# The feed-forward of an encoder layer in two stages, its inner activations passing through DRAM

## The reference

```python
x = x + gate1 * mix
h2 = rmsnorm(x, g_ffn) * (1 + scale2) + shift2
ff = (jax.nn.silu(h2 @ w_gate) * (h2 @ w_up)) @ w_down      # D_FF = 2816 = 22 tiles of 128
return x + gate2 * ff
```

## Time and profile before

| | |
|---|---|
| time, three runs | 1761.38, 1762.17 (median), 1762.43 us |
| the profiled execution | 1760.1 us, its span from first to last instruction 1758.3 us |
| mean granted TensorE clock | 0.999 of full speed |
| TensorE busy | 1718.3 us (98% of the span) |
| VectorE, ScalarE, GpSimd busy | 803.3, 440.5, 528.6 us |
| DRAM read, written | 98.51, 9.45 MB |

### The profile page before, as it was taken

How to read it: one execution, slowest core, us unless ns; L and a number is a source line. 1 busy time by engine, 2 the same in 40 slices (tenths; PEclk the granted TensorE clock), 3 DMA queues, 4 the chain that set the end, 5 groups by cost and what they waited for, 6 DMA issues and landing times.

```text
span 1758.3 us, 21827 instructions
## 1 busy us (share of the span) xinstructions
PE 1718.3 (98%) x8293; PEld 1370.7 (78%) x8293; DVE 803.3 (46%) x1235; ACT 440.5 (25%) x830; POOL 528.6 (30%) x431
## 2 busy tenths in 40 slices
PE   5999999999999999999999999999999999999998
PEld 1668888766768887888888888888888888888887
DVE  3705885078775364252515243242615243342525
ACT  4412332288761144101010111101010211111010
POOL 1301220188546553050504022040505031140505
PEclk9999999999999999999999999999999999999999
DMA  9751013154113101101100101110110101011013
GB/s 380 265 205 36 24 34 69 42 113 79 49 65 127 37 1 60 37 24 37 36 26 21 48 24 36 36 36 24 36 36 12 48 24 40 32 36 35 24 36 143
DMA packets 99311, 108.69 MB, mean 62 GB/s; under 512 B 19655, under 2 KB 82337, under 8 KB 95929
## 3 DMA queue, kind: packets, MB, share of 16 engines
q1 hardware_dynamic: 97401, 104.82, 19.0%
q10 hardware_dynamic: 1728, 3.15, 0.5%
q0 software_dynamic: 128, 0.02, 0.0%
HBM read 98.51 MB, written 9.45 MB: 61 GB/s over the span
## 4 chain that ended last, share of the span: by engine, by line
PE 78%; issue 1%; DVE 1%; ACT 0%; DMA 0%; POOL 0%; DVEq 0%; ACTq 0%; POOLq 0%
PE banks L101 23%; PE banks L102 23%; PE banks L103 23%; PE banks L989 2%; PE banks L1019 2%; PE banks L1325 2%; PE banks L998 2%; PE banks L1006 1%; PE banks L975 1%; PE banks L1790 1%; PE banks L1308 0%; DMA wff_raw<-in_w_up 0%; DVE alt L1231 0%; PE banks L1753 0%; PE banks L1336 0%
## 5 line engine op out<-in xcount | busy, mean ns | idle before, releaser
L1744 POOL TENSOR_TENSOR x<-x,ff_scratch 128x512 f32<-128x512 f32 x198 | 263.5, 1363 | 798.4 <-DVE ff_scratch L1636 797.8
L101 PE MATMUL banks<-h_hi,wff_hi 128*128 128x512 f32 x1056 | 411.5, 390 | 0.0
L103 PE MATMUL banks<-h_hi,wff_lo 128*128 128x512 f32 x1056 | 410.8, 389 | 0.0
L102 PE MATMUL banks<-h_lo,wff_hi 128*128 128x512 f32 x1056 | 410.8, 389 | 0.0
L1511 DVE TENSOR_TENSOR wff_lo<-wff_raw,wff_hi 128x1024 fp32r<-128x1024 f32 x66 | 81.6, 1236 | 403.7 <-ACT wff_hi L1507 403.7
L103 PEld LDWEIGHTS banks<-h_hi,wff_lo 128*128 128x128 f32 x1056 | 198.2, 188 | 41.3
L101 PEld LDWEIGHTS banks<-h_hi,wff_hi 128*128 128x128 f32 x1056 | 198.2, 188 | 41.0 <-issue 0.2
L102 PEld LDWEIGHTS banks<-h_lo,wff_hi 128*128 128x128 f32 x1056 | 198.2, 188 | 40.8
L1636 DVE TENSOR_TENSOR ff_scratch<-banks,gate 128x512 f32<-128x512 f32 x264 | 177.3, 687 | 73.8 <-PE banks L103 53.2
L101 PE MATMUL banks<-wff_hi,ff_hi 128*128 128x512 f32 x528 | 205.4, 389 | 0.0
L102 PE MATMUL banks<-wff_lo,ff_hi 128*128 128x512 f32 x528 | 205.4, 389 | 0.0
(11 more groups left out here) (173 smaller groups left out, 2096.1 us busy)
## 6 DMA issues: line engine op xcount, KB each, us to landing
ada_rest<-in_w_ada SPq DMA_DIRECT2D x16, 1024.0 KB, 7.0
wff_raw<-in_w_gate SPq DMA_DIRECT2D x22, 512.0 KB, 4.9
wff_raw<-in_w_up SPq DMA_DIRECT2D x22, 512.0 KB, 3.8
wff_raw<-in_w_down SPq DMA_DIRECT2D x22, 512.0 KB, 3.2
ada<-in_w_ada SPq DMA_DIRECT2D x8, 1024.0 KB, 16.3
win_raw<-in_w_in SPq DMA_DIRECT2D x16, 512.0 KB, 4.0
x_first<-in_x_sample SPq DMA_DIRECT2D x2, 2048.0 KB, 13.5
wo_raw<-in_w_o SPq DMA_DIRECT2D x4, 1024.0 KB, 5.0
```

Of the source, the lines that this page charges most:

```text
L101: pe.matmul(out, lhs[0], rhs[0], start=start, stop=False)
L102: pe.matmul(out, lhs[0], rhs[1], start=False, stop=False)
L103: return pe.matmul(out, lhs[1], rhs[0], start=False, stop=stop)
L1744: pool.tensor_tensor(part, part, scratch[:, n % 3], ALU.add).then_inc(d_added, 1)
```

## The change

The feed-forward is cut in two stages.

**Gate and up.** 22 units, gate and up of each pair in turn (`unit`). A unit covers two inner tiles: 256 columns of `w_gate` or `w_up`, loaded as one 1 MB transfer into one raw buffer, split in halves into one `a_hi`/`a_lo` buffer. Its six tiles (`ORDER`: both inner tiles of chunk 0, then of chunk 1, then of chunk 2) take banks 0 to 5. Silu goes to six slots in SBUF, the product replaces it in its slot, and SP stores the slot, 256 KB, in the new DRAM tensor `ff_rows` (2816 x 1536).

**Down.** 33 groups: for each chunk of 512 tokens the 11 pairs in turn (`down`). A group needs two row tiles of `w_down` and the two inner tiles of that chunk from `ff_rows`: three transfers of 512 KB (`load_down`) into one of three slots, which lie where `h_hi` and `h_lo` were. `down_hi` and `down_lo` split a slot in two instructions each, of 2048 and 1024 columns. The eight outputs of a chunk (four token tiles by two halves) hold the eight banks through all 11 groups of the chunk; each is gated and added to `x1` once, after the eleventh. SP loads group g + 3 when group g was used (`slot_used`). On VectorE the split of group g + 2 stands before the gating after group g. Outputs of a chunk are stored as halves (256 KB) during the next chunk, those of the last at the end. The down stage is written out, not looped.

Around it: the first weight tile's two splits stand elsewhere among the squares (ScalarE) and after tile 46 of `gate_mix` (VectorE); the third chunk's turns stand after each of the eight steps of the unit's second tile, in banks 6 and 7; `modulate` writes into the place of `h_lo` instead of a ring of two, which takes a wait out of it; semaphores of earlier stages are used again at higher counts.

```diff
...
+    ff_rows = nc.dram_tensor("ff_rows", (D_FF, T), F32).ap()
...
+    ORDER = [(f, c) for c in range(NCH) for f in range(2)]
...
+    f2_hi, f2_lo = (at(f"f2_{n}", [128, KT, T], F32R, off) for n, off in (("hi", H_HI), ("lo", H_LO)))
+    f2_raw = at("f2_raw", [128, KT, T], F32, H_LO)
...
+    DOWN_BANK = [6, 7, 0, 1, 2, 3, 4, 5]
...
+    def slot_used(eng, g):
+        c, jj = divmod(g, PAIRS)
+        if jj == PAIRS - 1:
+            eng.wait_ge(d_summed, DB * c + DB)
+        else:
+            eng.wait_ge(f2_used, (PAIRS - 1) * c + jj + 1)
...
+        def load_w(j, kind):
+            sp.dma_start(a_raw[:], (w_gate, w_up)[kind][:, bass.ds(j * 256, 256)].rearrange("(k p) n -> p k n", p=128)
+                         ).then_inc(raw_in, 16)
+        def load_next(j, kind):
+            u = 2 * j + kind
+            sp.wait_ge(w_ready, W0 + 2 * u + 2)
+            load_w(j + kind, 1 - kind)
+        def store_ff(j, i):
+            f, c = ORDER[i]
+            sp.wait_ge(product, 6 * j + i + 1)
+            sp.dma_start(ff_rows[bass.ds((2 * j + f) * 128, 128), CH * c:CH * c + CH], act_slot(i)).then_inc(ff_stored, 16)
+        def load_down(g):
+            c, jj = divmod(g, PAIRS)
+            s = g % 3
+            cols = slice(CH * s, CH * s + CH)
+            if g < 3:
+                sp.wait_ge(summed, done(PAIRS - 1, UP, 2 * s + 1))
+            else:
+                slot_used(sp, g - 3)
+            for f in range(2):
+                row = 128 * (2 * jj + f)
+                sp.dma_start(f2_raw[:, 2 * f:2 * f + 2, cols], w_down[row:row + 128, :].rearrange("p (h n) -> p h n", h=2)
+                             ).then_inc(f2_in[s], 16)
+            if c == 0:
+                sp.wait_ge(ff_stored, 96 * jj + 96)
+            sp.dma_start(f2_raw[:, 4:6, cols], ff_rows[256 * jj:256 * jj + 256, CH * c:CH * c + CH].rearrange(
+                "(f p) t -> p f t", p=128)).then_inc(f2_in[s], 16)
...
+        load_next(PAIRS - 1, GATE)
+        last = PAIRS - 1
+        store_ff(last, 0)
+        load_down(0)
+        store_ff(last, 1)
+        load_down(1)
+        for i in range(2, 5):
+            store_ff(last, i)
+        load_down(2)
+        store_ff(last, 5)
+        for g in range(3, GROUPS):
+            load_down(g)
...
+    def split_w_hi(act, j, kind, f):
+        act.wait_ge(raw_in, 16 * (2 * j + kind) + 16)
+        act.activation(a_hi[:, :, 128 * f:128 * f + 128], a_raw[:, :, 128 * f:128 * f + 128], ACT.Copy).then_inc(w_hi_s, 1)
+    def split_w_lo(dve, j, kind, f):
+        u = 2 * j + kind
+        dve.wait_ge(w_hi_s, W0 + 2 * u + f + 1)
+        dve.tensor_tensor(a_lo[:, :, 128 * f:128 * f + 128], a_raw[:, :, 128 * f:128 * f + 128],
+                          a_hi[:, :, 128 * f:128 * f + 128].bitcast(F32), ALU.subtract).then_inc(w_ready, 1)
+    def silu(act, j, i):
+        if i == 0 and not (isinstance(j, int) and j == 0):
+            act.wait_ge(ff_stored, 96 * j)
+        act.wait_ge(summed, done(j, GATE, i))
+        src = banks[:, i]
+        act.activation(act_slot(i), src, ACT.Silu).then_inc(silu_ready, 1)
+    def down_hi(act, g):
+        s = g % 3
+        cols = slice(CH * s, CH * s + CH)
+        act.wait_ge(f2_in[s], F2_IN0[s] + 48 * (g // 3) + 48)
+        act.activation(f2_hi[:, 0:4, cols], f2_raw[:, 0:4, cols], ACT.Copy).then_inc(f2_hi_s, 1)
+        act.activation(f2_hi[:, 4:6, cols], f2_raw[:, 4:6, cols], ACT.Copy).then_inc(f2_hi_s, 1)
+    def unit_act(act, j, kind, last):
+        for i in range(NP):
+            if kind == GATE:
+                silu(act, j, i)
+            if i >= NP - 2:
+                act.wait_ge(summed, done(j, kind, i))
+                if not last:
+                    split_w_hi(act, j + kind, 1 - kind, i - NP + 2)
+                else:
+                    down_hi(act, i - NP + 2)
...
-        split_hi(act, 0, 0)
...
+        act.wait_ge(o_summed, SEQ.index((2, TT - 1)) + 1)
+        split_w_hi(act, 0, GATE, 0)
         square(8)
-        square(9)
-        square(10)
-        split_hi(act, 0, 1)
-        square(11)
+        split_w_hi(act, 0, GATE, 1)
+        for t in range(9, 12):
+            square(t)
...
+        for g in range(2, GROUPS):
+            down_hi(act, g)
...
+    def down_lo(dve, g):
+        s = g % 3
+        cols = slice(CH * s, CH * s + CH)
+        for i, part in enumerate((slice(0, 4), slice(4, 6))):
+            dve.wait_ge(f2_hi_s, 2 * g + i + 1)
+            dve.tensor_tensor(f2_lo[:, part, cols], f2_raw[:, part, cols], f2_hi[:, part, cols].bitcast(F32), ALU.subtract
+                              ).then_inc(f2_ready, 1)
+    def unit_dve(dve, j, kind, last):
+        for i in range(NP):
             if kind == UP:
+                dve.wait_ge(summed, done(j, kind, i))
+                dve.wait_ge(silu_ready, SILU0 + 6 * j + i + 1)
+                dve.tensor_tensor(act_slot(i), banks[:, i], act_slot(i), ALU.mult).then_inc(product, 1)
+            if i >= NP - 2:
                 if not last:
+                    split_w_lo(dve, j + kind, 1 - kind, i - NP + 2)
+                else:
+                    down_lo(dve, i - NP + 2)
...
+            if m == TT * OS - 2:
+                split_w_lo(dve, 0, GATE, 0)
+        split_w_lo(dve, 0, GATE, 1)
...
+        for g in range(GROUPS):
+            if g + 2 < GROUPS:
+                down_lo(dve, g + 2)
+            c, jj = divmod(g, PAIRS)
+            if jj < PAIRS - 1:
+                continue
+            dve.wait_ge(gate2_in, 16)
+            for n in range(DB):
+                m = DB * c + n
+                t, half = divmod(m, 2)
+                cols = slice(512 * half, 512 * half + 512)
+                dve.wait_ge(d_summed, m + 1)
+                if m >= 3:
+                    waits_added(dve, m - 3)
+                dve.tensor_tensor(scratch[:, m % 3], banks[:, DOWN_BANK[n]], gate2[:, REQ[c], cols], ALU.mult).then_inc(d_gated, 1)
+                if on_dve(n):
+                    dve.wait_ge(d_gated, m + 1)
+                    dve.tensor_tensor(x1_back[:, t, cols], x1_back[:, t, cols], scratch[:, m % 3], ALU.add).then_inc(d_added_dve, 1)
...
+        def unit(j, kind):
+            u = 2 * j + kind
+            first = isinstance(u, int) and u == 0
+            for i, (f, c) in enumerate(ORDER):
+                if c == 0:
+                    pe.wait_ge(w_ready, W0 + 2 * u + f + 1)
+                if first:
+                    if i < 4:
+                        pe.wait_ge(gated, TT * OS - 3 + i)
+                    else:
+                        pe.wait_ge(t_ready, TURN0 + KT * 2)
                     if f == 0:
+                        h_ready(c)
+                elif kind == GATE:
+                    pe.wait_ge(product, 6 * (j - 1) + i + 1)
+                else:
+                    pe.wait_ge(silu_ready, SILU0 + 6 * j + i + 1)
+                for k in range(KT):
+                    last = mm3(pe, banks[:, i], [part[:, k, 128 * f:128 * f + 128] for part in (a_hi, a_lo)],
+                               [part[:, k, CH * c:CH * c + CH] for part in (h_hi, h_lo)], k == 0, k == KT - 1)
+                    if k == KT - 1:
+                        last.then_inc(summed, 1)
+                    if first and i == 1:
+                        turn(2 * KT + k)
+        def down(g):
+            c, jj = divmod(g, PAIRS)
+            s = g % 3
+            cols = slice(CH * s, CH * s + CH)
+            pe.wait_ge(f2_ready, 2 * g + 2)
+            for n in range(DB):
                 t, half = divmod(n, 2)
+                bank = DOWN_BANK[n]
+                if jj == 0 and c:
+                    pe.wait_ge(d_gated, DB * (c - 1) + n + 1)
+                elif jj == 0 and n >= 2:
+                    pe.wait_ge(product, 6 * (PAIRS - 1) + n - 1)
                 for f in range(2):
+                    last = mm3(pe, banks[:, bank], [part[:, 4 + f, CH * s + 128 * t:CH * s + 128 * t + 128] for part in (f2_hi, f2_lo)],
+                               [part[:, 2 * f + half, cols] for part in (f2_hi, f2_lo)], jj == 0 and f == 0, jj == PAIRS - 1 and f == 1)
+                if jj == PAIRS - 1:
+                    last.then_inc(d_summed, 1)
+            if jj < PAIRS - 1:
+                last.then_inc(f2_used, 1)
...
+        for g in range(GROUPS):
+            down(g)
...
```

More of the change, by code:

```diff
@@ L1396, in second_half @@
[L1396 to L1399, removed]
+    o_summed, gated, x1_added = sem("o_summed"), sem("o_gated"), sem("x1_added")
+    squared, rooted, rstd, xn_dve, xn_act = kept.squared_act, kept.rooted, kept.rstd_ready, kept.x_normed, sem("xn_act")
+    turned, t_ready, hi_ready, split_even, split_odd = (
+        kept.x_turned, kept.t_ready, kept.h_hi_ready, kept.split_even, kept.split_odd)
@@ L1484, in run_sp @@
             load_o(n)
-        load(0, 0)
-        sp.wait_ge(o_summed, TT * OS)
-        load(0, 1)
-        sp.wait_ge(gated, TT * OS)
-        load(0, 2)
```

(35 more changed lines are left out.)

412 lines of the change are left out of this document (152 added, 260 removed).

## The result

The changed kernel takes **1770.24 us** (median of 7 runs, 1766.26 to 1774.64) against 1761.66 us for the kernel before beside it (7 runs, 1760.09 to 1762.43): ratio 1.0047, 95% interval 1.0034 to 1.006. It is slower by 8.6 us. The forecast was 1767.0 us in a range of 1761.5 to 1771.0. Timed again later it took 1767.61 us against 1761.77 (5 runs; 1.0034, interval 1.002 to 1.0048).

The account below looks back on a forecast made before the run. TensorE's matmul stream was taken to set the end. Terms +5.2 (stops), +0.3 (gate-up to down), -0.2 (start), -0.5 (tail) gave +4.8 on the profiled 1760.1; with the median 2.1 higher, 1767.0 us, range 1761.5 to 1771.0.

Parts of the forecast that it names:

- Matmuls: Feed-forward on TensorE: 4752 matmuls of the same shapes at the same pitch, 1077.2 us as before, cost 0.
- removed work: Gatings and residual additions fall from 264 to 24 each; no TensorE wait names them, so gain 0.
- steady groups: Down stage inside a chunk: load, split and subtractions take 12.5 us of 21.8 available, hidden, cost 0.
- The stops: After groups 10 and 21, TensorE waits 2.5 us for gating behind loads and split; 2.6 each with restart, +5.2.
- the restart: TensorE's first matmul after a stop: 0.32 us instead of 0.23 to the second, a tenth more per stop.
- The clock behind the stops: Down stage after each chunk end: no prediction step had slow matmuls there; only the restart's tenth was priced.
- From gate-up to down: Between the stages: first group's split takes 5.42 us, TensorE comes after 5.25; with a restart +0.3 us.
- The start: First feed-forward matmul through first turn: 0.4 late plus 1.4 idle less 2.0 of present waits, -0.2 us.
- The waits behind `t_second`: TensorE waits of 0.6 us at the third chunk's turns, said to go: no ring, no silu in between.
- The tail: Kernel's end: last store is 256 KB instead of 512, 2.1 against 2.6 us, so -0.5 us.
- loads land sooner: Rival at chunk ends: loads of 5.95 us, deciding below 6.4; sum +2.5, 1764.7 us, no change; chance 0.25.
- No stops: Rival at chunk ends: gating not last, or split in time; with start's waits gone -2.5, 1759.7 us; chance 0.10.

Follow-up runs that it names:

- the filled stop: Changed kernel plus twelve matmuls with a stationary tile of zeros at the first and second chunk ends; 1765.51 us against 1767.61 for the changed kernel beside it.
- the run with two landings: Changed kernel, but the split's first part waits only for the two `w_down` loads, its second for the inner tiles' load; 1762.06 us, ratio 1.0003 to before.
- the gate-first kernel: Changed kernel with VectorE gating before splitting group g + 2 at both chunk ends: 1760.20 us; with the first weight's subtraction one tile earlier too: 1759.42 us.

## Why the prediction came out as it did

The direction and the mechanism were right: two stops, after groups 10 and 21, by the order on VectorE. Its steps in turn:

- **Matmuls, removed work, steady groups**: right. The pitch is 0.2267 us as before, the changed kernel waits in no other place, and the 4752 matmuls cost the same. 407 us less work on VectorE and GpSimd bought nothing, since no wait of TensorE hung on it.
- **The stops**: forecast 2.6 each with the restart, 5.2 together; measured 2.17 + 2.81 = 4.98. The loads of 6.74 and 7.38 us bracket the 7.07 taken from the loads of `x`.
- **The clock behind the stops**: missing. The restart was priced at a tenth of a microsecond an end, from the row of a turn, behind which the clock had not fallen; it cost 1.69 and 1.49 us here, and the filled stop, together with the DMA shares of the other stretches, shows that this is the stop's doing. The Trainium skill ("TensorE: Matmul & The Clock Gate", HAM oscillation) says that TensorE's standing still makes the clock drop in a running kernel. The trace agrees in three of the four stops of the changed kernel's two profiles, though the waits in the page's example are longer than these. It should have stood among the rivals.
- **From gate-up to down**: right, forecast +0.3, measured +0.30.
- **The start**: mis-sized. Forecast -0.2, measured 0.25 + 0.11 - 1.62 = -1.26. The waits behind `t_second` went, as said. TensorE started 0.36 later instead of 0.4: the subtraction ended at 672.10, 1.1 us after the GpSimd instruction that was running (to 671.01), so VectorE was next, as forecast, and not GpSimd's addition. But the wait at the first turn came out at 0.97 us instead of the 1.4 that were put there, and other small gaps among the turns went too.
- **The tail**: right, forecast -0.5, measured -0.58.

With the forecast's own terms the sum was +4.8; corrected by +3.2 for the clock, -0.2 for the stops, -1.1 for the start and -0.1 for the tail it is the 6.6 us of the profile. Two errors of opposite sign, +3.2 and -1.1, partly cancelled; that the sum is better than its parts is luck. The median of the first seven runs is 3.2 us above the forecast, that of the second five 0.6; how much of this is the scatter of the part ahead and how much the clock behind the stops was read in two profiles only.

Of the rivals, "loads land sooner" would have needed less than 6.4 us; the rows gave 6.7 to 8.6, and the run with two landings shows what it would have brought. "No stops" is the gate-first kernel: 1.2 us faster than before by the medians (interval to no difference at all), where the rival said 2.5. In its profile the start gives 1.26 us and the tail some 0.6, with 0.30 lost from gate-up to down; that is 1.6, and no other place of its feed-forward differs from before. The gate-first kernels are the best of this study, and hold at most 0.2% over the kernel before.

## What to carry to other kernels

On an engine that works in program order, hand the next consumer its buffers first and prefetch afterwards: the same instructions in the other order at two places out of 33 were worth 8 us here. When TensorE sets the time, a stop can cost more than its length (here up to 2.7 us of slow matmuls behind it), so look at the granted clock of the stretch behind it and not only at the waits. Work taken from engines that TensorE doesn't wait for is worth nothing until a wait names it.

## What was not expected of the hardware

- After stops of 2.17, 2.52, 2.81, 4.02 and 5.46 us between dense matmuls the granted clock was half for some microseconds (matmul pitch 0.43 instead of 0.23 us); after stops of 0.75 to 1.55, and after one of 2.39, it stayed at full.
- Twelve multiplications by zeros in place of the stop went with full clock behind both ends, and with 24 matmuls more in it the feed-forward was shorter from first to last matmul: 1087.56 us against 1090.33 and 1088.84. The medians, 1765.51 against 1767.61 us, point the same way, but the runs overlap.
- At the chunk ends three 512 KB loads issued in a row, with little else in the queue, took 6.7 to 8.6 us to the reader's start, and two of them 5.3.
